# Choosing experts ahead of prompt attention, with four or five slot pairs of each chunk moved into it

## The chip, the cores and the metric

The kernel runs on one core of a Trainium2 chip. The metric is device time in microseconds, the median of three timed executions. Beside them stands one execution taken with the hardware profiler, from which all rows below come. Engine names are those of the profile: PE is TensorE, PEld its weight loads, DVE is VectorE, ACT is ScalarE, POOL is GpSimd (here it only issues DMAs), SP is SyncE (it issues the weight tiles and other large loads).

## The reference

One decoder layer over 1024 prompt tokens and 8 x 4 new tokens. What matters here is its last part, a retrieval of experts for each token:

```python
q = (xb @ w_query).reshape(PEER_BLOCK, PEER_HEADS, PEER_KEY_DIM)        # 8 heads
s1 = einsum('thd,hkd->thk', q[..., :half], sub_keys[:, 0])              # 128 scores
s2 = einsum('thd,hkd->thk', q[..., half:], sub_keys[:, 1])              # 128 scores
v1, i1 = top_k(s1, 16); v2, i2 = top_k(s2, 16)
cand = v1[..., :, None] + v2[..., None, :]                              # 256 candidates
sv, si = top_k(cand, 16)
eidx = take_along_axis(cidx, si)                                        # 16 experts
gate = softmax(sv)
act = gelu(einsum('thkd,td->thk', expert_u[eidx], xb))
out = einsum('thk,thkd->td', gate * act, expert_v[eidx])
```

Ahead of it stand one combined input projection, differential attention (8 heads, causal), an S5 state-space branch with a gated linear unit, two gated projections, an output projection, and rmsnorms. All is float32.

## The kernel before

**Chunks and stages.** After a front part (norm, S5 scan) the tokens are taken in three chunks: blocks 0 and 1; blocks 2 to 4; blocks 5 to 7 with the new tokens. A chunk runs through the stages glu, s5, v, att, dec (the last chunk alone), ga, out and query. In chunk 0 attention comes first and has no retrieval beside it. Each stage is a block of its own: all engines meet at its end. glu, s5, ga and query multiply weight tiles of 128x1024 (8 or 16 a stage, loaded by SP) with the chunk's 384 or 416 columns.

**Retrieval beside the stages.** Blocks 0, 1, 2, 3, the new tokens, 6 and 7 are "gathered". For each of 50 "heads" (a block's head g) 16 slots are worked off in 8 pairs, 400 pairs in all. A slot is one expert row per token: POOL gathers 128 rows of 8 KB (1 MB) into a ring of 8 buffers, DVE makes the dot product (`u_dot`, L1130), ACT the gelu and the weight (L1221, L1230), and DVE adds the weighted row (`v_add`, L1140). `dve_step(p)` does the two dots of pair p and the two additions of pair p-1. Blocks 4 and 5 are worked densely in a last stage, over all 128 x 128 experts, with the pairs from 240 on beside it.

**Where the pairs lie.** `PAIR_PLAN` says how many pairs each stage takes, by an order written by hand; `share` spreads them over the steps of the stage. After unit n of attention (one head of attention and one block of 128 queries; 24 units a chunk) the pairs up to `27 * (n + 2) // 24` of the stage have been done in chunk 1, so that some units take two pairs and the others one. In glu and s5 the pairs up to `n_pairs * (j + 1) // 8` come ahead of DVE's product for tile or tile pair j.

**Choices.** Before the slots of head g can be gathered, DVE must choose its 16 experts (`choose`, `top_pairs`, parts 0 to 5, a chain of 13 links, L1047 to L1093). Head g+2 is chosen beside the pairs of head g, part r behind pair 8g + r:

```python
if r < 6 and g + 2 < HEADS:
    choose(dve, g + 2, r)
```

The results (idx, tops, gates, gsum, ntop) lie in buffers of 4 heads. POOL loads the scores of head g from DRAM 8 pairs ahead of its choice (`step_scores`, `load_scores`).

**Attention on DVE and ACT.** In unit n DVE makes the probabilities (L1834, L1836, L1840), the first dot and addition of its pair (`begin_pair`), the maxima of the next unit (L1827), and then the rest of its pair or pairs; at the middle unit of each head of attention in chunks 1 and 2 it also normalises the head before (L1851, L1853). ACT takes in the output of the unit before (L1739), copies the turned probabilities (L1776), makes the next unit's exponentials (L1731), the roots (L1750), takes in a key or query tile (L1712, L1716), and then the pairs' gelus and weights.

Of the kernel before, what the change touches and what calls it, by code (L numbers as in the profile page):

```python
# [15 lines left out]
U32 = mybir.dt.uint32  # L16
# [28 lines left out]
ARENA = 52992  # L45
# [11 lines left out]
def hybrid_step(nc, dr, out):  # L57

    root = ExitStack()
    with root:  # L60
# [418 lines left out]
        with nc.Block() as block:  # L479
# [138 lines left out]
            def _(sp):  # L618
# [9 lines left out]
                for b in range(2):  # L628
# [11 lines left out]
                     (7, 14, 9, 27, 0, 14, 7, 18),  # L640
                     (8, 15, 10, 28, 40, 15, 8, 16))
# [204 lines left out]
        RING, AHEAD, KCH = 8, 6, 13  # L846
# [95 lines left out]
        for g in range(2, HEADS):  # L942
            assert scores_kept(g) or step_scores(g) <= HALF * (g - 2), (g, step_scores(g))
# [40 lines left out]
        def gather(pool, s):  # L984
# [3 lines left out]
            if s >= RING:  # L988
# [3 lines left out]
                                    bass.IndirectOffsetOnAxis(ap=idx[:, g % 4, j:j + 1], axis=0)  # L992
# [31 lines left out]
        def head_job(g):  # L1024
            return g + sum(step < HALF * (g - 2) for step in DENSE_STEP)

        def dense_job(d):
            return d + DENSE_STEP[d] // HALF + 3
# [51 lines left out]
        def choose(dve, g, part):  # L1080
            if part < 5:
# [9 lines left out]
                top_pairs(dve, head_job(g), part, mine, tops[:, g % 4, :], e12)  # L1091
            else:
                nc.vector.scalar_tensor_tensor(idx[:, g % 4, :], e12[:, 0, :], float(PK), e12[:, 1, :],  # L1093
# [24 lines left out]
        def gate_norm(dve, g):  # L1118
            dve.wait_ge(ex_d, g + 1)
            nc.vector.reciprocal(gsum[:, g % 4:g % 4 + 1], gsum[:, g % 4:g % 4 + 1]).then_inc(gt_v, 1)  # L1120
# [56 lines left out]
        def dve_step(dve, p):  # L1177
# [12 lines left out]
            if r < 6 and g + 2 < HEADS:  # L1190
                choose(dve, g + 2, r)
# [7 lines left out]
        def gate_exp(act, g):  # L1199
            act.wait_ge(tk_done, g + 1)  # L1200
            nc.scalar.activation(ntop[:, g % 4:g % 4 + 1], tops[:, g % 4, 0:1], ACT.Copy, scale=-1.0).then_inc(nt_d, 1)
            act.wait_ge(nt_d, g + 1)
            nc.scalar.activation(gates[:, g % 4, :], tops[:, g % 4, :], ACT.Exp, bias=ntop[:, g % 4:g % 4 + 1],
                                 accum_out=gsum[:, g % 4:g % 4 + 1]).then_inc(ex_d, 1)

        def gate_scale(act, g):
            act.wait_ge(gt_v, g + 1)
            nc.scalar.activation(gates[:, g % 4, :], gates[:, g % 4, :], ACT.Copy, scale=gsum[:, g % 4:g % 4 + 1]).then_inc(gs_d, 1)
# [1586 lines left out]
```

## Time and profile before

| | |
|---|---|
| median of 3 runs | 4130.23 us (4128.51 to 4132.54) |
| profiled execution | 4135.06 us, of which the span from first to last instruction is 4133.2 us |
| mean granted TensorE clock | 0.909 |
| PE busy | 3444.7 us (83%) |
| DVE busy | 3099.4 us (75%) |
| ACT busy | 1516.5 us (37%) |
| mean DMA rate | 317 GB/s |
| gathers of expert rows (L991) | 800 |

A share of busy time is a mean over stages with different limits, so the table says little on the stages that the change touches; the rows further down are by stage. The stages' bounds in the trace, in microseconds: glu of chunk 1 from 742 to 796.8, s5 to 900.3, v to 953.9, attention to 1208.3, ga to 1315.3, out to 1383.8, query to 1517.3; chunk 2: glu to 1571.7, s5 to 1682.8, v to 1743.8, attention to about 2031. The dense tiles run from 3094 to the end at 4133.2.

### The profile page before, as it was taken

Reading aid. Unit: us, or ns where it says so; the run is one execution under the profiler, and the core shown is the slowest. Engines: PE = TensorE matmul, PEld = TensorE weight load, DVE = VectorE, ACT = ScalarE, POOL = GpSimd, SP = SyncE. Lnnn points to the kernel's source line nnn. Section 1 sums busy time; section 2 is a strip of 40 time slices with the busy share of each in tenths; the row PEclk is TensorE's granted clock in tenths of the full one; section 3 lists DMA queues with packets and bytes.
Section 4 is the critical chain, followed back from the end, with each engine's and each line's share of the span. In section 5 each row is a group of like instructions: output and inputs, shape, how many; then the busy total and the mean of one; then the engine's idle time right before and its main releaser. Section 6 shows DMA issues by size and latency. Waiting matters only on the chain. (4 is left out here: it accounts for less than half of the span.)

```text
span 4133.2 us, 48907 instructions
## 1 busy us (share of the span) xinstructions
PE 3444.7 (83%) x15862; PEld 2286.7 (55%) x15862; DVE 3099.4 (75%) x6443; ACT 1516.5 (37%) x3644; POOL 1057.2 (26%) x880
## 2 busy tenths in 40 slices
PE   7988997887778688888677848884779999999998
PEld 5756875544444344355466634343436666666665
DVE  6584112788978778889876878899978887788775
ACT  2232521434763234266533323323433333233232
POOL 0100001332223333412222233332323333332331
PEclk9999998998989889998887869897989999999999
DMA  3032456998879999978798979987999999999996
GB/s 140 4 97 99 140 174 248 352 418 318 318 267 416 353 390 389 412 259 287 273 388 338 362 303 387 333 323 246 376 354 370 416 416 416 415 416 417 413 412 243
DMA packets 312800, 1311.93 MB, mean 317 GB/s; under 512 B 39586, under 2 KB 115842, under 8 KB 206178
## 3 DMA queue, kind: packets, MB, share of 16 engines
q0 software_dynamic: 120320, 854.80, 52.5%
q1 hardware_dynamic: 191842, 453.87, 29.4%
q8 instruction: 128, 2.10, 0.2%
q14 instruction: 126, 1.03, 0.1%
q10 hardware_dynamic: 384, 0.13, 0.0%
HBM read 1250.07 MB, written 56.79 MB: 316 GB/s over the span
## 5 line engine op out<-in xcount | busy, mean ns | idle before, releaser
L991 POOL DMA_INDIRECT arena<-in_uv,arena x800 | 1001.4, 1252 | 2324.9 <-DVE arena L1140 2088.4
L695 PE MATMUL ps<-arena 128*128 128x256 f32 (+2 forms) x3456 | 1107.0, 480 | 148.4 <-DMA arena<-in_w_stat 69.6
L1130 DVE CUSTOM_DVE_ANT_0 arena<-arena 128x1024 f32<-128x1024 f32 x800 | 972.7, 1219 | 52.2 <-DMA arena<-in_uv,arena 35.7
L1140 DVE SCALAR_TENSOR_TENSOR arena<-arena 128x1024 f32<-128x1024 f32 x736 | 942.5, 1281 | 86.9 <-ACT arena L1230 86.0
L695 PEld LDWEIGHTS ps<-arena 128*128 128x128 f32 x3456 | 676.3, 199 | 535.5 <-issue 361.4
L1221 ACT ACTIVATE arena<-arena 128x2 f32<-128x2 f32 x400 | 81.0, 203 | 1136.8 <-DVE arena L1130 1095.9
L2542 PE MATMUL ps<-arena 128*128 128x256 f32 x2048 | 470.9, 384 | 0.0
L2551 PE MATMUL ps<-arena 128*128 128x512 f32 x1024 | 460.1, 592 | 0.5 <-DMA arena<-in_uv 0.5
L2542 PEld LDWEIGHTS ps<-arena 128*128 128x128 f32 x2048 | 385.2, 193 | 48.9 <-issue 0.5
L2551 PEld LDWEIGHTS ps<-arena 128*128 128x128 f32 x1024 | 194.4, 190 | 192.2 <-issue 185.8
L2656 DVE TENSOR_TENSOR arena<-arena 128x256 f32<-128x256 f32 x128 | 79.8, 624 | 253.1 <-ACT arena L2621 222.2
L1221 ACT ACT_TABLE_LOAD x138 | 177.1, 1283 | 56.2 <-PEq L1394 23.3
L1230 ACT ACTIVATE arena<-arena 128x1 f32<-128x1 f32 x800 | 192.0, 287 | 13.5 <-ACT arena L1221 0.6
L2531 PEld LDWEIGHTS ps<-ident,arena 128*128 128x128 f32 x1024 | 121.0, 143 | 109.9 <-issue 81.4
L2531 PE MATMUL ps<-ident,arena 128*128 128x128 f32 x1024 | 136.9, 278 | 39.4 <-ACT arena L2596 22.9
L2244 PE MATMUL ps<-arena 128*128 128x512 f32 (+1 forms) x288 | 129.6, 611 | 24.9 <-PEq L1394 14.5
L2596 ACT ACTIVATE arena<-ps 128x512 f32<-128x512 f32 x256 | 135.9, 580 | 33.6 <-PE ps L2531 19.6
L1982 PE MATMUL ps<-arena 128*64 128x128 f32 x1024 | 145.5, 303 | 0.0
L1827 DVE TENSOR_REDUCE arena<-ps 128x1 f32<-128x384 f32 (+5 forms) x128 | 90.8, 751 | 68.6 <-PE ps L1640 68.3
L2021 PE MATMUL ps<-ident,arena 128*128 128x128 f32 x512 | 83.8, 311 | 69.9 <-DMA arena<-in_cache_k 40.9
L1982 PEld LDWEIGHTS ps<-arena 128*64 128x64 f32 x1024 | 129.4, 154 | 13.6 <-issue 10.5
L307 PE MATMUL ps<-arena 128*128 128x512 f32 (+1 forms) x288 | 126.2, 600 | 4.2 <-PEq L118 4.2
(296 smaller groups left out, 4101.5 us busy)
## 6 DMA issues: line engine op xcount, KB each, us to landing
arena<-in_uv SPq DMA_DIRECT2D x256, 512.0 KB
arena<-in_w_stat SPq DMA_DIRECT2D x216, 512.0 KB
arena<-in_cache_k SPq DMA_DIRECT2D x64, 512.0 KB
arena<-in_cache_v SPq DMA_DIRECT2D x64, 512.0 KB
arena<-in_w_mov SPq DMA_DIRECT2D x14, 2048.0 KB, 13.1
scr_w<-arena SPq DMA_DIRECT2D x16, 1024.0 KB, 19.6
arena<-scr_w SPq DMA_DIRECT2D x16, 1024.0 KB
arena<-in_uv,arena POOLq DMA_INDIRECT x800
```

Source lines behind the costliest of these rows:

```text
L695: last = nc.tensor.matmul(ps[:, bank, 0:w], wbuf[m % NWB][:, kc * P:(kc + 1) * P], moving[:, kc, :], start=(kc == 0), stop=(kc == KC - 1))
L991: pool.indirect_dma_start(ring[s % RING], None, dr["uv"], bass.IndirectOffsetOnAxis(ap=idx[:, g % 4, j:j + 1], axis=0)).then_inc(row_in[s ...
L1130: nc.vector.tensor_tensor_reduce(ring[s % RING][:, 0:D], ring[s % RING][:, 0:D], h2r[:, b % 2, :], 1.0, 0.0, ALU.mult, ALU.add, act_in[:, ...
L1140: nc.vector.scalar_tensor_tensor(accr[:, b % 2, :], ring[s % RING][:, D:2 * D], wgt[:, s % RING:s % RING + 1], accr[:, b % 2, :], ALU.mult ...
L1221: nc.scalar.activation(act_out[:, p % 2, :], act_in[:, k:k + 2], ACT.Gelu).then_inc(gelu_d, 1)
L1230: last = nc.scalar.activation(wgt[:, k + q:k + q + 1], gates[:, g % 4, 2 * r + q:2 * r + q + 1], ACT.Copy, scale=act_out[:, p % 2, q:q + 1])
L1982: last = nc.tensor.matmul(flat_s[:, p * P:(p + 1) * P], qpad[:, h * ROWS:(h + 1) * ROWS], kT[:, n % 2, h, :], start=(h == 0), stop=(h == H ...
L2244: last = nc.tensor.matmul(ps[0:rows, 2 * (b % 2) + k, :], mT[:, kc, (b - b0) * P:(b - b0) * P + rows], o_slab[:, k, kc, :], start=(kc == 0 ...
L2531: last = nc.tensor.transpose(ps[:, 6 + i // 4, (i % 4) * P:(i % 4 + 1) * P], u_rows[:, e % NUR, i * P:(i + 1) * P], ident[:, :])
L2542: last = nc.tensor.matmul(ps[:, 4 + e % 2, 0:2 * P], u_turned[:, e % 2, kc, :], h2d[:, kc, :], start=(kc == 0), stop=(kc == KC - 1))
L2551: last = nc.tensor.matmul(ps[:, 2 * j + k, :], wgt_t[:, e % NW, j * P:(j + 1) * P], v_rows[:, e % NV, 512 * k:512 * (k + 1)], start=(e == ...
L2596: nc.scalar.activation(u_turned[:, e % 2, 4 * i:4 * i + 4, :].rearrange("p c n -> p (c n)"), ps[:, 6 + i, :], ACT.Copy).then_inc(turn_free, 1)
```

## The change

The plan moves pairs and choices; no operation is added or left out. In chunk 1 glu, s5, v and ga take one pair less each and attention four more; in chunk 2 glu takes one less, s5 two, v one, and attention four more. The boundaries before chunk 1's glu (4), at chunk 1's end (100), after chunk 2's attention (161) and at the end of chunk 2 (240) stay.

Each choice now takes four successive pairs rather than six (`CHOICE_PARTS`), from a step given by `CHOICE_STEP`. For heads 2 to 10 and 15 to 22 the steps are written out, for the others they are 8(g-2) as before. So heads 3 to 8 are all chosen between pairs 6 and 29, ahead of chunk 1's attention (pairs 31 to 61), heads 9 and 10 in ga; heads 15 to 21 between pairs 100 and 127, ahead of chunk 2's attention (129 to 160), and head 22 from its last pair on. Results are kept for 8 heads, the ring of diagonal matrices (`diag`, used by pairs 240 to 271) shrinks from 4 to 3, and scores are loaded 6 pairs ahead of their choice.

```diff
-ARENA = 52992
+ARENA = 53040
...
         PAIR_PLAN = ((0, 0, 0, 0, 0, 0, 0, 4),
-                     (7, 14, 9, 27, 0, 14, 7, 18),
-                     (8, 15, 10, 28, 40, 15, 8, 16))
+                     (6, 13, 8, 31, 0, 13, 7, 18),
+                     (7, 13, 9, 32, 40, 15, 8, 16))
...
-        RING, AHEAD, KCH = 8, 6, 13
+        RING, AHEAD, KCH, CHOSEN, NDIAG = 8, 6, 13, 8, 3
...
-        idx, tops, gates, gsum = take([4, TOPK], U32), take([4, TOPK]), take([4, TOPK]), take([4])
-        ntop = take([4])
+        idx, tops, gates, gsum = take([CHOSEN, TOPK], U32), take([CHOSEN, TOPK]), take([CHOSEN, TOPK]), take([CHOSEN])
+        ntop = take([CHOSEN])
...
-        diag, spread, ss8 = take([4, P]), take([NS]), take([1])
+        diag, spread, ss8 = take([NDIAG, P]), take([NS]), take([1])
...
+        CHOICE_PARTS = ((0,), (1,), (2, 3), (4, 5))
+        BEFORE_ATT = (0, 6, 10, 14, 18, 22, 26, 62, 66), (100, 104, 108, 112, 116, 120, 124, 160)
+        CHOICE_STEP = [-2, -1] + [HALF * (g - 2) for g in range(2, HEADS)]
+        CHOICE_STEP[2:11], CHOICE_STEP[15:23] = BEFORE_ATT
+
         def step_scores(g):
-            return (-2, -1, -1)[g] if g < 3 else max(HALF * (g - 3), PAIRS_BEFORE[chunk_of(GATHERED[head_block(g)]) + 1])
+            return (-2, -1, -1)[g] if g < 3 else max(CHOICE_STEP[g] - 6, PAIRS_BEFORE[chunk_of(GATHERED[head_block(g)]) + 1])
...
         def head_job(g):
-            return g + sum(step < HALF * (g - 2) for step in DENSE_STEP)
+            return g + sum(step < CHOICE_STEP[g] for step in DENSE_STEP)
...
-            if r < 6 and g + 2 < HEADS:
-                choose(dve, g + 2, r)
+            for n in range(2, HEADS):
+                if 0 <= p - CHOICE_STEP[n] < len(CHOICE_PARTS):
+                    for part in CHOICE_PARTS[p - CHOICE_STEP[n]]:
+                        choose(dve, n, part)
...
                         n = v_before_pe[p] + q
-                        if n >= 4:
-                            act.wait_ge(v_pe, n - 3)
-                        nc.scalar.activation(diag[:, n % 4, 0:m], pattern, ACT.Copy, scale=wgt[:, k + q:k + q + 1]).then_inc(diag_d, 1)
+                        if n >= NDIAG:
+                            act.wait_ge(v_pe, n - NDIAG + 1)
+                        nc.scalar.activation(diag[:, n % NDIAG, 0:m], pattern, ACT.Copy, scale=wgt[:, k + q:k + q + 1]).then_inc(diag_d, 1)
```

## Rows read from the trace of the kernel before

**Rows 1.** Windows by stage: bounds and length, busy us by engine, PEclk, DMA share, GB/s

```profile
751.30:796.80 45.50, 35.48 (x111) 20.56 (x109) 44.32 (x81) 28.89 (x48) 18.93 (x15) 0.91 0.93 369
796.80:900.30 103.50, 91.31 (x257) 52.35 (x258) 83.12 (x147) 39.32 (x78) 36.64 (x30) 0.91 0.97 391
900.30:953.90 53.60, 41.31 (x96) 18.00 (x96) 51.79 (x95) 14.11 (x43) 25.91 (x19) 0.93 1.01 408
953.90:1208.30 254.40, 189.00 (x816) 120.34 (x816) 216.09 (x422) 170.66 (x385) 57.23 (x57) 0.86 0.83 296
1208.30:1315.30 107.00, 86.91 (x256) 50.12 (x257) 89.53 (x165) 36.85 (x73) 36.96 (x31) 0.91 0.92 371
1526.60:1571.70 45.10, 38.40 (x110) 20.54 (x109) 43.16 (x80) 27.28 (x44) 18.86 (x15) 0.95 1.00 403
1571.70:1682.80 111.10, 96.10 (x257) 51.24 (x257) 91.18 (x164) 38.90 (x80) 38.95 (x32) 0.91 0.97 392
1682.80:1743.80 61.00, 57.17 (x128) 22.23 (x129) 59.18 (x105) 22.83 (x58) 29.94 (x23) 0.97 1.01 412
1743.80:2031.00 287.20, 229.98 (x1101) 152.65 (x1101) 248.46 (x441) 191.71 (x389) 60.45 (x61) 0.89 0.78 276
3094.00:4133.20 1039.20, 1006.02 (x4083) 694.40 (x4081) 786.64 (x1361) 317.03 (x868) 313.80 (x250) 0.99 0.97 394
```

**Rows 2.** DVE's waits: glu 1, s5 1, ga 1, glu 2, s5 2 (us, times, longest)

```profile
DVE arena L1381 <- ACT arena L1373: 9.5, 1, 9.5
...
DVE arena L1445 <- PE ps L695: 13.2, 3, 7.7
DVE arena L1130 <- DMA arena<-in_uv,arena: 5.3, 7, 1.2
...
DVE arena L1447 <- PE ps L695: 8.1, 2, 7.8
DVE arena L1130 <- DMA arena<-in_uv,arena: 7.8, 5, 2.8
...
DVE arena L1381 <- ACT arena L1373: 2.3, 1, 2.3
...
DVE arena L1130 <- DMA arena<-in_uv,arena: 10.1, 8, 2.4
```

**Rows 3.** Timeline of DVE: one pair, then a choice, then the next

```profile
2787.70 1.23 DVE L1130 CUSTOM_DVE_ANT_0 arena<-arena 128x1024 f32<-128x1024 f32 x1
...
2792.39 0.48 DVE L1047 MAX8 arena<-arena 128x8 f32<-128x128 f32 x2
...
2794.61 0.09 DVE L1058 MATCH_VALUE_LOAD arena<-arena 128x8 f32 x1
...
2798.05 0.17 DVE L1069 TENSOR_SCALAR arena<-arena 128x16 uint32<-128x16 uint32 x1
...
2800.73 0.49 DVE L1047 MAX8 arena<-arena 128x8 f32<-128x128 f32 x2
```

**Rows 4.** Windows of single attention heads, two of chunk 1, one of chunk 2

```profile
1026.60:1061.50 34.90, 24.54 (x96) 16.17 (x98) 32.20 (x63) 21.27 (x50) 8.43 (x8) 0.81 0.84 294
1061.50:1084.70 23.20, 21.62 (x106) 13.60 (x102) 21.80 (x39) 19.58 (x43) 4.69 (x5) 0.99 0.88 315
1831.70:1859.60 27.90, 25.80 (x138) 17.15 (x136) 25.41 (x40) 21.37 (x41) 4.68 (x5) 1.00 0.81 285
```

**Rows 5.** Timeline of DVE and ACT, a middle unit without choice, chunk 2

```profile
1841.37 1.22 DVE L1130 CUSTOM_DVE_ANT_0 arena<-arena 128x1024 f32<-128x1024 f32 x1
...
1850.71 0.18 DVE L1851 RECIPROCAL arena<-arena 128x3 f32<-128x3 f32 x1 [2.25 <-ACT arena L1750]
...
1851.10 1.28 ACT L1221 ACT_TABLE_LOAD   x1
1852.40 0.20 ACT L1221 ACTIVATE arena<-arena 128x2 f32<-128x2 f32 x1
1852.63 0.48 ACT L1230 ACTIVATE arena<-arena 128x1 f32<-128x1 f32 x2
```

More of the change, by code:

```diff
@@ L942, in hybrid_step @@
         for g in range(2, HEADS):
-            assert scores_kept(g) or step_scores(g) <= HALF * (g - 2), (g, step_scores(g))
+            assert scores_kept(g) or step_scores(g) <= CHOICE_STEP[g], (g, step_scores(g))
+            assert (g == 2 or CHOICE_STEP[g - 1] + len(CHOICE_PARTS) <= CHOICE_STEP[g]) and CHOICE_STEP[g] <= HALF * (g - 1) - 2 and g - CHOICE_STEP[g] // HALF < CHOSEN
         def load_scores(pool, g):
@@ L1024, in head_job @@
         def head_job(g):
-            return g + sum(step < HALF * (g - 2) for step in DENSE_STEP)
+            return g + sum(step < CHOICE_STEP[g] for step in DENSE_STEP)
         def dense_job(d):
-            return d + DENSE_STEP[d] // HALF + 3
+            return d + sum(step <= DENSE_STEP[d] for step in CHOICE_STEP)
         assert sorted([head_job(g) for g in range(HEADS)] + [dense_job(d) for d in range(2 * PH)]) == list(range(HEADS + 2 * PH))
@@ L1090, in choose @@
                     dve.wait_ge(loaded, n)
-                top_pairs(dve, head_job(g), part, mine, tops[:, g % 4, :], e12)
+                top_pairs(dve, head_job(g), part, mine, tops[:, g % CHOSEN, :], e12)
             else:
-                nc.vector.scalar_tensor_tensor(idx[:, g % 4, :], e12[:, 0, :], float(PK), e12[:, 1, :],
+                nc.vector.scalar_tensor_tensor(idx[:, g % CHOSEN, :], e12[:, 0, :], float(PK), e12[:, 1, :],
                                                ALU.mult, ALU.add).then_inc(tk_done, 1)
@@ L1200, in gate_exp @@
             act.wait_ge(tk_done, g + 1)
-            nc.scalar.activation(ntop[:, g % 4:g % 4 + 1], tops[:, g % 4, 0:1], ACT.Copy, scale=-1.0).then_inc(nt_d, 1)
+            nc.scalar.activation(ntop[:, g % CHOSEN:g % CHOSEN + 1], tops[:, g % CHOSEN, 0:1], ACT.Copy, scale=-1.0).then_inc(nt_d, 1)
             act.wait_ge(nt_d, g + 1)
-            nc.scalar.activation(gates[:, g % 4, :], tops[:, g % 4, :], ACT.Exp, bias=ntop[:, g % 4:g % 4 + 1],
-                                 accum_out=gsum[:, g % 4:g % 4 + 1]).then_inc(ex_d, 1)
+            nc.scalar.activation(gates[:, g % CHOSEN, :], tops[:, g % CHOSEN, :], ACT.Exp, bias=ntop[:, g % CHOSEN:g % CHOSEN + 1],
+                                 accum_out=gsum[:, g % CHOSEN:g % CHOSEN + 1]).then_inc(ex_d, 1)
         def gate_scale(act, g):
             act.wait_ge(gt_v, g + 1)
-            nc.scalar.activation(gates[:, g % 4, :], gates[:, g % 4, :], ACT.Copy, scale=gsum[:, g % 4:g % 4 + 1]).then_inc(gs_d, 1)
+            nc.scalar.activation(gates[:, g % CHOSEN, :], gates[:, g % CHOSEN, :], ACT.Copy, scale=gsum[:, g % CHOSEN:g % CHOSEN + 1]).then_inc(gs_d, 1)
         def act_step(act, p):
@@ L1229, in act_step @@
                 for q in range(2):
-                    last = nc.scalar.activation(wgt[:, k + q:k + q + 1], gates[:, g % 4, 2 * r + q:2 * r + q + 1], ACT.Copy,
+                    last = nc.scalar.activation(wgt[:, k + q:k + q + 1], gates[:, g % CHOSEN, 2 * r + q:2 * r + q + 1], ACT.Copy,
                                                 scale=act_out[:, p % 2, q:q + 1])
@@ L1272, in pe_step @@
                 for c in range(2):
-                    last = nc.tensor.matmul(ps[0:m, 6 + c, :], diag[:, n % 4, 0:m],
+                    last = nc.tensor.matmul(ps[0:m, 6 + c, :], diag[:, n % NDIAG, 0:m],
                                             ring[s % RING][:, D + 512 * c:D + 512 * (c + 1)],
```

4 lines of the change are left out of this document (2 added, 2 removed).

## The prediction

> **What bounds the kernel now.** I read the page first (PE 83%, DVE 75%, both means over unlike stages), then windows cut at the bounds of the stages, then the waits of DVE in them, and at last the timeline of attention, unit by unit. In the windows [rows 1] three things are to be seen. The dense tiles from 3094 on are PE's: 1006.0 of 1039.2 us busy. No pair is moved into or out of them, so I take them as fixed, with all from pair 161 on. Second, from glu of chunk 1 to v of chunk 2, DVE is busy 80 to 97% of each stage and the DMA engines move 370 to 412 GB/s at a share near 1. Third, attention runs the DMA engines at 0.83 and 0.78 and DVE at 85 and 87%. So there is room for transfers in attention, and hardly any on DVE ahead of it.
>
> Every stage ends with a meeting of all engines, so the last engine sets each stage by itself. In glu and v that is DVE: glu of chunk 1 is 44.3 of 45.5 us busy after its first tile. In s5 and ga DVE is also last, but idles 20.4 and 17.5 us [rows 1]: for the first product of PE (part of 13.2 and 8.1 us) and for gathered rows (5.3, 7.8 and, in s5 of chunk 2, 10.1 us) [rows 2].
>
> **The prices.** A pair is 4.69 us of DVE when nothing holds it (2787.70 to 2792.39). A choice is 8.34 us (2792.39 to 2800.73): 2.2 for part 0, 3.4 for parts 1 and 2, 2.7 for 3 to 5 [rows 3]. The choices of gathered heads add part 5, one small operation; I take 8.4. Both DVE totals stay; only their place changes, and with it what hides them.
>
> **The change, stage by stage** (from the lists of pairs and choice steps of either plan).
> - Query of chunk 0: the last parts of head 2 now come behind pair 3, ahead of the block's end: +1.9 us.
> - Glu 1: one pair less; choices 8.4 for the 7.9 before. DVE is the last engine, and PE, 35.5 us busy in the same stretch, leaves room: -4.2.
> - s5 1: one pair less (-4.7), choices 27.4 where there were 13.4 (+14.0). Of this the first part 0 (2.2) now lies in the wait for the first product, and DVE's other waits, 5.5 for PE and 5.3 for rows, mostly go (8.4 of 10.8): -1.3. If none went it would be +7.1.
> - v 1: -4.7 and +4.7: 0.
> - ga 1: one pair less, choices +8.8 (head 9 whole, part 3 of head 11), 2.2 of it in the first wait, and of 7.8 us for rows I take half away: -2.0; with all waits kept +1.9.
> - Query 1: head 14 is ended there, behind its last pair and with DVE the last engine: +1.5.
> - Glu 2: this is the surprise. With 8 pairs, `share` puts one ahead of the first product, where DVE waits only 2.3 us more; with 7 it puts none there (7 // 8 = 0), and DVE waits some 9.5 as in glu 1 [rows 2]. Behind the first product stand 7 pairs in both plans, but 14.5 us of choices for 6.2: +8.3.
> - s5 2: two pairs less (-9.4), choices +11.2; of the 10.1 us for rows I take 6.6 away: -4.8, with waits kept +1.8.
> - v 2: -4.7 and +5.7: +1.0.
>
> **Attention** decides the rest. It loses 27.9 us of choices in chunk 1 (from part 3 of head 6 to head 9; part 2 lay in the wait before the first maxima) and 25.2 in chunk 2, and gets four pairs in each. By DVE's sum that is -9.1 and -6.4. But a head without choices is not DVE's alone: 23.2 us with DVE 21.8 and PE 21.6 busy in chunk 1, 27.9 with 25.4 and 25.8 in chunk 2 [rows 4]. PE and ACT are at their limit too, and choices now fill waits. The extra pairs become second pairs of a unit. In a middle unit of chunk 2 the probabilities are done at 1841.37, and ACT has its exponentials, roots and a query tile to do before it can load the gelu table at 1851.10 and give the weights at 1852.63 + 0.48 [rows 5]. The first addition of a second pair waits for these weights. It can start at 1853.3; two additions, a dot and the 2.3 us from L1851 to the next first dot (row 1850.71, whose wait of 2.25 us is then gone) put the next unit at 1859.2, where it was 1853.05. So a second pair in a middle unit costs 6.1 us, not 4.7. The same reckoning gives 6.0 for middle units of chunk 1, 5.9 for first and 5.0 for last ones.
>
> In chunk 1 the second pairs rise from 3 to 7, net 22.9 us. A head with one second pair (5.9) and 6.1 us of choices takes 34.9 us, 11.7 over the free one [rows 4]: there a choice gave 0.95 of its length, so 26.5 go: -4 (bounds -9 and +3). In chunk 2 `32 * k // 24` puts all second pairs into middle units, one a head where every other head had one: 4 x 6.1 = +24.4. A choice there fills first what the free head idles (2.5 us), so I take 0.7 of its length: 25.2 x 0.7 = 17.6. That is +7 (bounds -6 and +11).
>
> On the price of the table load the Trainium skill (ScalarE: Activation LUTs, What ACT_TABLE_LOAD costs) says about 1283 ns plus some 1380 ns of drain for each change of set. The trace agrees on the first and shows no drain: the load at 1851.10 takes 1.28 and the gelu starts at 1852.40 [rows 5]. By the page each of the 8 new second pairs would wait 1.4 us longer, +11 us in all; the row decides.
>
> **What I cost at nothing.** Attention's first wait (part 2 of head 6 lay in it). Scores loaded 6 instead of 8 pairs ahead, and only 4 ahead for head 16 and 2 for head 3, whose choices come early: POOL issues them ahead of that step's gathers, and at 5 us a pair or more 2 pairs are 10 us; cover gone, DVE would wait once or twice some 5 us. POOL's wait for choices gets shorter, since every choice ends earlier. Three diagonals for four: ACT waits for PE at most a pair earlier, in a stretch where PE takes them microseconds later; 0 to +2. Choices in four steps instead of six elsewhere: same work.
>
> **Sum.** +1.9 -4.2 -1.3 +0 -2.0 +1.5 +8.3 -4.8 +1.0 is +0.4 outside attention, -4 and +7 in it: +3.4 us. The profiled execution's 4135.1 (span 4133.2 and 1.9 around it) becomes 4138.5; it lies 4.8 over the median of 4130.2, which becomes **4133.6**.
>
> **The rivals.**
> - *Attention is DVE's after all.* Second pairs cost 4.7 and choices give all back: -9.1 and -6.4 where I have -4 and +7, so 18.5 less: 4115. For it: DVE is 94% busy in the free head of chunk 1. Against: the 2.25 us wait.
> - *Bytes rule ahead of attention.* Eight pairs leave the stages ahead of it, at 2.1 MB each and 0.41 MB/us 5.1 us apiece: -41, and attention takes them into its free DMA time: about 4090. For it: the share near 1 [rows 1]. Against: DVE waited for rows only 5 to 10 us a stage [rows 2]. The Trainium skill (Perfetto Trace Analysis, Optimization Strategy) says that interleaving regimes with different most-contended engines can improve performance; here that would be this case.
> - *A second pair costs more* (slower). If ACT gives the weights 1.8 us later than reckoned, since PE's tile is late at a lower clock (0.81 in the head of 34.9 us, 0.99 in the free one [rows 4]), eight new ones bring +14: 4148. With my sum at +3.4 it decides from some 6.6 us a second pair on.
> - *The relief does not come* (slower). DVE gets 34.0 us more of choices in both s5 and ga, and its waits for rows and PE stay: 8.4, 6.6 and 3.9 over my terms: 4152. It decides from 5 of these 19 us on.
> - *Nothing to be seen*: my sum is itself within 0.2% (8.3 us), about what a measurement of this kernel can tell from no change, so this is no case apart.
>
> **How the numbers follow.** My sum 0.49 (of it 0.40 within 0.2%, 0.05 faster, 0.04 slower); DVE's attention 0.20 (0.18 faster); bytes 0.06; dearer second pairs 0.14 (0.12 slower); no relief 0.11 (0.10 slower). That is faster 0.29, same 0.45, slower 0.26. The range takes in the first and third rival, 4111 to 4149; my sum alone would be 4123 to 4144.
>
> **What would show it.** Attention of chunk 1 near 250 us and of chunk 2 near 294 (254.4 and 287.2 now); a wait of L1140 for ACT L1230 in nearly every unit with two pairs, none of 2.25 us at L1851; glu 2 near 63 us with a wait of about 9 us at L1381; s5 2 near 106 with under 4 us for rows. Attention of chunk 2 under 283 us would prove me wrong on second pairs, s5 2 over 111 on the relief.

## The result and the profile after

The changed kernel takes 4183.93 us (median of 4 runs, 4172.27 to 4193.32), the kernel before 4131.39 in the same comparison (4128.51 to 4138.27): a ratio of 1.0116, 95% interval 1.0097 to 1.0135. It is slower by 1.2%, where I forecast 4133.6 and a range up to 4149. The profiled execution is the slowest of the four, 4193.3 us with a span of 4191.5, against 4133.2 before. (Four pairs of each chunk go into attention, 27 to 31 and 28 to 32, not "four or five" as the title has it.)

Windows of the changed kernel at the bounds of its stages (columns as in [rows 1]; glu, s5, v, attention and ga of chunk 1, query of chunk 1, then glu, s5 and v of chunk 2):

```profile
738.30:789.70 51.40, 43.04 (x128) 25.04 (x129) 40.45 (x79) 27.43 (x45) 17.55 (x15) 0.93 0.93 368
789.70:890.60 100.90, 89.39 (x256) 51.41 (x257) 91.20 (x199) 36.95 (x73) 34.70 (x29) 0.92 0.96 386
890.60:945.60 55.00, 43.62 (x96) 18.94 (x97) 51.71 (x104) 13.88 (x41) 20.78 (x16) 0.90 0.94 340
945.60:1215.80 270.20, 195.06 (x817) 124.55 (x817) 207.26 (x335) 173.66 (x397) 70.86 (x64) 0.84 0.85 307
1215.80:1316.60 100.80, 86.69 (x257) 50.09 (x257) 92.66 (x194) 37.40 (x71) 35.03 (x29) 0.94 0.92 371
1384.50:1524.10 139.60, 103.22 (x353) 63.97 (x353) 105.83 (x190) 31.24 (x88) 55.54 (x41) 0.87 1.00 389
1524.10:1585.90 61.80, 47.79 (x128) 25.49 (x128) 50.86 (x113) 30.80 (x50) 19.88 (x17) 0.86 0.86 331
1585.90:1690.40 104.50, 95.84 (x257) 51.05 (x257) 91.52 (x191) 39.99 (x76) 35.72 (x29) 0.94 0.93 372
1690.40:1752.10 61.70, 56.94 (x128) 22.21 (x129) 58.54 (x122) 15.52 (x45) 23.47 (x18) 0.97 0.94 344
```

The stages outside attention sum to little, as forecast: 4.2 us less from query of chunk 0 to v of chunk 2. Attention of chunk 1 grew from 254.4 [rows 1] to 270.2. Chunk 2's attention has no clean bound in the trace, so I compare both from the first unit's probabilities to the last unit's. The kernel before:

```profile
973.00:1196.40 223.40, 167.99 (x752) 107.63 (x752) 206.36 (x401) 161.69 (x364) 54.61 (x55) 0.88 0.84 302
1764.10:2020.20 256.10, 207.45 (x1026) 138.74 (x1026) 239.73 (x427) 182.97 (x370) 58.35 (x59) 0.90 0.79 277
```

The changed kernel:

```profile
964.10:1203.90 239.80, 174.79 (x752) 112.18 (x752) 199.27 (x321) 164.59 (x375) 67.39 (x62) 0.86 0.86 312
1772.70:2053.20 280.50, 219.24 (x1026) 149.37 (x1026) 238.07 (x356) 198.26 (x394) 74.41 (x65) 0.86 0.80 282
```

The case is in these four lines. DVE has less to do in both (199.3 for 206.4, 238.1 for 239.7), as my sum had it, and yet they are 16.4 and 24.4 us longer. DVE waits more. And the 1026 products of PE in chunk 2's line take 219.2 us instead of 207.5, at a granted clock of 0.86 instead of 0.90: the same work has grown.

Where the profiled executions differ, in us (after minus before): ahead of the change -3.4; stages outside attention as far as v of chunk 2 -4.2; attention of chunk 1 +15.9; attention of chunk 2 +24.4 and decode +3.2; ga, out and query of chunk 2 up to pair 240 +4.5; pairs 248 to 274 +17.8; everything behind 0. That is 58.2 of a difference of 58.3 in the spans. Pairs 248 to 274 lie beside the grid stage, the one ahead of the dense tiles, in which results of ACT are stored into the DRAM tensor scr_w.

DVE's waits in chunk 2 between those bounds, before:

```profile
DVE arena L1140 <- ACT arena L1230: 7.6, 8, 2.1
DVE arena L1851 <- ACT arena L1750: 4.5, 2, 2.3
```

and after (lines moved by 6 and 8):

```profile
DVE arena L1146 <- ACT arena L1238: 34.4, 15, 3.7
DVE arena L1842 <- ACT arena L1739: 5.0, 12, 1.5
```

The additions wait 26.8 us more for ACT's weights. Every middle unit of chunk 2 now has two pairs: 8 units, where the kernel before had 4 (in chunk 1 it is 7 for 3). One of them, DVE:

```profile
1856.12 1.29 DVE L1146 SCALAR_TENSOR_TENSOR arena<-arena 128x1024 f32<-128x1024 f32 x1 [1.10 <-ACT arena L1238]
1857.43 2.36 DVE L1835 TENSOR_REDUCE arena<-ps 128x1 f32<-128x1024 f32 x2
...
1867.01 1.29 DVE L1146 SCALAR_TENSOR_TENSOR arena<-arena 128x1024 f32<-128x1024 f32 x1 [3.66 <-ACT arena L1238]
...
1872.94 1.22 DVE L1136 CUSTOM_DVE_ANT_0 arena<-arena 128x1024 f32<-128x1024 f32 x1
```

and ACT beside it:

```profile
1862.53 0.20 ACT L1739 ACTIVATION_READ_ACCUMULATOR arena<-ps,arena 128x1 f32 x1
...
1863.04 1.28 ACT L1758 ACT_TABLE_LOAD   x1
1864.33 0.21 ACT L1758 ACTIVATE arena<-arena 128x3 f32<-128x3 f32 x1
1864.44 0.50 ACT L1724 ACTIVATE arena<-ps 128x416 f32<-128x416 f32 x1
1864.96 1.28 ACT L1229 ACT_TABLE_LOAD   x1
1866.25 0.20 ACT L1229 ACTIVATE arena<-arena 128x2 f32<-128x2 f32 x1
1866.49 0.48 ACT L1238 ACTIVATE arena<-arena 128x1 f32<-128x1 f32 x2
```

From the maxima (1857.43) to the next unit's dot (1872.94) are 15.51 us. In the free unit of the kernel before the maxima start at

```profile
1843.71 2.35 DVE L1827 TENSOR_REDUCE arena<-ps 128x1 f32<-128x1024 f32 x2
```

and the prediction put the next dot at 1859.2 with a second pair, so 15.5 us. That part of the reckoning held to 0.1 us. The Trainium skill's drain behind a table load (ScalarE: Activation LUTs, What ACT_TABLE_LOAD costs), which by its figure would have made it an estimated 1.4 us more, is again not there: load at 1864.96, gelu at 1866.25. What I had missed lies around it. Windows of the changed kernel over another head's two-pair unit (1925.7 to 1944.8), its beginning and its last part, and over the unit behind it:

```profile
1925.70:1930.00 4.30, 4.30 (x24) 2.56 (x22) 3.06 (x6) 2.97 (x8) 0.71 (x1) 1.00 1.05 370
...
1940.00:1944.80 4.80, 0.93 (x8) 0.52 (x4) 4.28 (x8) 4.45 (x11) 2.10 (x2) 0.80 0.46 155
1944.80:1953.30 8.50, 5.70 (x26) 5.33 (x27) 8.24 (x15) 4.71 (x8) 1.92 (x3) 0.51 0.81 307
```

and PE's longest wait in the head from 1907.7 on:

```profile
PE ps L1670 <- DVE arena L1848: 5.6, 1, 5.6
```

While DVE waits for weights and makes up the second pair, PE has no new probabilities to turn (transpose, L1670): it idles 5.6 us at a stretch (0.9 us busy of the last 4.8). Behind that idle stretch the granted clock falls from 1.00 to 0.51, which is its lower level of 1.2 GHz nearly throughout, and the next unit starts with slow products. The same eight turning products take 1.97 us there and 1.04 in the free head before; and in the middle unit of the next head ACT, which has to take in PE's key or query tile ahead of the gelu, waits for it:

```profile
1837.48 1.97 PE L1670 MATMUL ps<-ident,arena 128*128 128x128 f32 x8 [5.57 <-DVE arena L1848]
1853.54 0.52 ACT L1720 ACTIVATE arena<-ps 128x416 f32<-128x416 f32 x1 [1.09 <-PE ps L695]
```

```profile
1853.43 1.04 PE L1662 MATMUL ps<-ident,arena 128*128 128x128 f32 x8
```

(The first two are the changed kernel's, the last is the free head's.) PE begins the products of that tile 3.55 us into the head, where it was 2.23 in the free one, and the difference of 1.3 us is handed on to ACT and to DVE's first addition, the 1.10 us above. In the free head before, the clock stayed at 1.00 and PE had 25.8 of 27.9 us to do [rows 4]; now a head of chunk 2 takes 36.1 us on the mean, and PE is 30.4 us busy in the one from 1907.7 to 1944.8. So the second pair costs 8.2 us over a free head: the 6.1 of the reckoning, some 1.3 in its own unit (1.10 ahead of the first addition) and 0.8 in the two others. How much of these 2.1 us is the idle stretch itself and how much the low clock behind it, the runs don't separate.

### The profile page after: what moved, and what is told of

The parts are those of the page before. It is cut to its first block and busy times, and to the rows that moved or that the text cites. A ratio compares the mean times of both kernels' runs of the same rounds, so it can differ in the third digit from the quotient of the medians.

```text
span 4191.5 us, 48844 instructions
## 1 busy us (share of the span) xinstructions
PE 3473.5 (83%) x15862; PEld 2312.9 (55%) x15862; DVE 3103.0 (74%) x6443; ACT 1525.7 (36%) x3649; POOL 1081.2 (26%) x880
## 5 line engine op out<-in xcount | busy, mean ns | idle before, releaser
L997 POOL DMA_INDIRECT arena<-in_uv,arena x800 | 1025.2, 1281 | 2361.3 <-DVE arena L1146 2122.6
L1229 ACT ACT_TABLE_LOAD x141 | 180.9, 1283 | 62.1 <-PEq L1402 32.2
L2029 PE MATMUL ps<-ident,arena 128*128 128x128 f32 x512 | 83.9, 312 | 66.8 <-DMA arena<-in_cache_k 36.9
## 6 DMA issues: line engine op xcount, KB each, us to landing
arena<-in_w_mov SPq DMA_DIRECT2D x14, 2048.0 KB, 13.6
arena<-in_uv,arena POOLq DMA_INDIRECT x800, 10.8
```

Source lines behind the costliest of these rows:

```text
L997: pool.indirect_dma_start(ring[s % RING], None, dr["uv"], bass.IndirectOffsetOnAxis(ap=idx[:, g % CHOSEN, j:j + 1], axis=0)).then_inc(row_ ...
L1229: nc.scalar.activation(act_out[:, p % 2, :], act_in[:, k:k + 2], ACT.Gelu).then_inc(gelu_d, 1)
```

## The experiments

The table has the lengths that the texts below speak of, from one profiled execution each: attention from first to last probabilities, the stages ahead (chunk 1: glu, s5, v, ga; chunk 2: glu, s5, v) and query 1, in us. The medians of the kernel before lay between 4129.7 and 4134.4 us in the different comparisons; the ratios are to the one of the same comparison.

| kernel | attention 1 | attention 2 | ahead, chunk 1 | query 1 | ahead, chunk 2 | median, ratio to before (95%) |
|---|---|---|---|---|---|---|
| before | 223.4 | 256.1 | 318.5 | 133.5 | 226.5 | |
| choices alone | 211.2 | 249.8 | 327.7 | 139.4 | 238.4 | 4151.7, 1.0039 (1.0021 to 1.0058) |
| pairs alone | 255.4 | 294.1 | 299.0 | 133.0 | 209.7 | 4163.1, 1.0071 (1.0043 to 1.0099) |
| changed | 239.8 | 280.5 | 308.1 | 139.6 | 228.0 | 4183.9, 1.0116 (1.0097 to 1.0135) |
| changed, gelu earlier | 220.9 | 258.7 | 307.5 | 142.0 | 223.0 | 4143.5, 1.0007 (0.9987 to 1.0027) |
| pairs alone, gelu earlier | 244.6 | 278.5 | 297.9 | 132.5 | 210.8 | 4141.1, 1.0015 (1.0002 to 1.0029) |
| before, gelu earlier | 220.2 | 251.8 | 317.9 | 130.0 | 225.0 | 4130.6, 0.9984 (0.9966 to 1.0002) |
| one pair a unit | 201.2 | 230.0 | 331.9 | 134.0 | 226.8 | 4110.9, 0.9943 (0.9922 to 0.9963) |

### The two halves of the change

Choices alone is the changed kernel with the old plan of pairs; pairs alone is the kernel before with the new one.

```diff
-                     (6, 13, 8, 31, 0, 13, 7, 18),
-                     (7, 13, 9, 32, 40, 15, 8, 16))
+                     (7, 14, 9, 27, 0, 14, 7, 18),
+                     (8, 15, 10, 28, 40, 15, 8, 16))
```

> The changed kernel with the old plan of pairs: only the choices are moved (and the three diagonals kept). Theory 1, cover: a choice beside a second pair lay in the wait of the first addition for ACT's weights and was nearly free there, so taking it out gives little: attention of chunk 2 falls only some 7 us (287.2 to about 280), that of chunk 1 some 16 (254.3 to about 238); the stages ahead of them gain some 28 us over the changed kernel; with the 20 us of the stretch of pairs 240 to 272 the total is about 4155. Theory 2, the prediction's 0.95 and 0.7 of a choice: attention falls by 26 and 18 us (to 228 and 270), total about 4135.

> The kernel before with the new plan of pairs: the choices stay beside the pairs of head g-2. Theory 1, cover: a second pair costs some 8.5 us in a unit whether or not choices lie there, and the choices lie in the wait, so attention comes out about as in the changed kernel or 0 to 10 us a chunk longer (270 to 280 and 311 to 322). Theory 2, the prediction's sum: a second pair costs 6.1 and the choices come on top: 254.3 + 23 = 277 and 287.2 + 24 = 311. What tells them apart is the difference to the changed kernel in chunk 2's attention: 18 us by theory 2, under 8 by theory 1. Glu of chunk 2 near 62 us by both. Total about 4165 (theory 1), 4172 (theory 2).

Windows of choices alone:

```profile
983.90:1195.10 211.20, 165.41 (x752) 107.06 (x752) 180.84 (x296) 161.44 (x364) 53.90 (x54) 0.91 0.87 315
1781.20:2031.00 249.80, 205.22 (x1026) 136.97 (x1026) 216.88 (x327) 182.96 (x369) 58.73 (x56) 0.92 0.80 285
```

Windows of pairs alone:

```profile
953.10:1208.50 255.40, 176.66 (x752) 113.45 (x752) 230.99 (x453) 164.84 (x375) 65.19 (x63) 0.84 0.82 294
1754.10:2048.20 294.10, 217.63 (x1026) 149.13 (x1026) 264.92 (x468) 198.14 (x394) 71.64 (x68) 0.84 0.78 272
```

Both halves cost time, and together they cost what they cost singly. Taking the choices out gives 12.2 us in chunk 1 and 6.3 in chunk 2 at the old plan, and 15.6 and 13.6 at the new one. Their DVE time is 27.9 and 25.2 us, so about half comes back at best and a quarter at worst. Four pairs more cost 32.0 and 38.0 us where choices lie beside them, and 28.6 and 30.7 where none do: 7.2 to 9.5 us each. Theory 1 had choices alone right (a stage of 242.0 us for its 238; the stretch from v's end to pair 161's first dot 289.8 for before's 296.5); in pairs alone it was too strong: that stretch is 333.4, 12.5 us over the changed kernel's 320.9, between its 8 and theory 2's 18.

The cover of theory 1 can be read head by head. In chunk 2 of the kernel before, three heads have a second pair and 6.4 to 6.9 us of choices each; they take 36.7, 36.9 and 38.1 us, and with the choices moved away 35.0, 34.8 and 35.0. So a choice there gave back 0.3 to 0.5 of its length, and the middle units themselves, 54.5 us in all, became 55.3. Over chunk 2's attention the wait for the weights grows from 7.6 to 21.5 us where DVE's work falls by 22.9:

```profile
DVE arena L1146 <- ACT arena L1238: 21.5, 12, 3.7
```

But it depends on the place in the unit. In pairs alone three middle units have their choice (2.2 us) only behind the second pair, after the wait; there the wait is 3.66 us as in the changed kernel, and they take 21.25 us where the changed kernel takes 19.03: the choice comes on top in full. Only what lies ahead of the second pair's first addition can fill the wait. These three units are 6.7 of the 13.6 us that the choices gave beside the new plan, where they gave 6.3 beside the old.

Ahead of attention pairs alone wins 36.3 us over the stages of the table, a mean of 4.5 for each of the eight pairs. The mean hides a spread: one pair less gave 4.3 us in glu 1, 8.5 in s5 1, 2.3 in ga 1 and nothing in glu 2, and two gave 12.8 in s5 2, where DVE's waits for rows fell from 10.1 to 1.1 us and those for PE rose from 7.8 to 19.1. So in s5 a pair is worth more than DVE's 4.69 us, and these stages are not shown to be DVE's alone. Choices alone loses 9.2 + 5.9 + 11.9 = 27.0 us there, and 18.5 come back in attention: a choice is dearer where it goes than where it leaves.

Glu of chunk 2 is a clean check of one term: 61.8 us in the changed kernel, 62.1 with the choices alone, 54.8 with the pairs alone (54.5 before). The pair that leaves it brings nothing, as its place is taken by a wait; the choices bring all of the 7.3.

### ACT gives the weights earlier

In a unit with two pairs ACT works the first of them off right behind the exponentials, ahead of the roots and the key or query tile.

```diff
+                        if share(c, "att", n + 1, N) - done_pairs["act"] == 2:
+                            peer_act(act, done_pairs["act"] + 1)
                         if rooted(n) is not None:
                             roots(rooted(n))
```

> The changed kernel, but in a unit with two pairs ACT does the gelu and the weights of the first of them right behind the exponentials, ahead of the roots and of the key or query tile. Theory 1: the weights come 2.1 us earlier in the middle units of chunk 2, the wait of 3.7 us ahead of the second pair's first addition falls to about 1.5, the stretch to pair 161 falls by 8 x 2 = 16 us, attention of chunk 1 by 5 to 12; total 4155 to 4165. Theory 2 (what waits is only moved, since PE gets its key and query tiles taken in later and the roots come later): within 5 us.

Waits of DVE between the probabilities of chunk 2's first and last unit:

```profile
DVE arena L1146 <- ACT arena L1238: 16.0, 14, 1.8
```

Windows, same bounds as above:

```profile
967.80:1188.70 220.90, 169.65 (x752) 109.64 (x752) 198.70 (x320) 167.93 (x378) 67.49 (x62) 0.89 0.91 337
1756.10:2014.80 258.70, 208.59 (x1026) 137.48 (x1026) 236.73 (x355) 203.34 (x398) 74.33 (x65) 0.93 0.85 306
```

Timeline of a middle unit, DVE and ACT:

```profile
1834.97 2.36 DVE L1837 TENSOR_REDUCE arena<-ps 128x1 f32<-128x1024 f32 x2
...
1840.57 1.28 ACT L1229 ACT_TABLE_LOAD   x1
...
1842.62 1.28 DVE L1146 SCALAR_TENSOR_TENSOR arena<-arena 128x1024 f32<-128x1024 f32 x1 [1.74 <-ACT arena L1238]
```

Theory 1 holds and is outdone: 40 us, where I expected some 25. The weights come 7.65 us behind the maxima instead of 9.58, the wait falls from 3.66 to 1.74, and with PE idle for less time the clock is 0.93 instead of 0.86 and PE's 1026 products take 208.6 us again, not 219.2. DVE's work in the stretch is unchanged within 1.4 us. The edit is a swap in one engine's order. It adds a table load to units in which the second gelu would have found its table loaded (65 loads for 61 in the stretch, ACT 203.3 us busy for 198.3); ACT has the time.

The same edit on the kernel before and on pairs alone tells whether the choices had been cover:

> The kernel before with the earlier gelu on ACT in units with two pairs (3 in chunk 1, 5 in chunk 2), nothing else. Theory 1: of the some 20 us that the edit took from each attention of the changed kernel, with 7 and 9 such units, it takes as much for each such unit here, 2.2 to 2.7 us: 18 to 20 us in all, 4112 to 4116 where the kernel before has 4132. Theory 2, cover: here half of the units with two pairs have choices, which fill the wait for the weights, and the edit brings only what waits are left (L1140 for L1230, 0.5 to 2.1 us a unit in the rows): 8 units by about 1, total 4122 to 4128.

> The new plan of pairs with the choices where they were and with the earlier gelu. Theory 1 (ACT's late weights made a second pair dear): with them early it costs some 5 us, so attention comes to about 264 and 300 to pair 161 (286.3 and 333.4 without), against 38 us won ahead of it; total 4163 - 38 = 4125. Theory 2, cover: the choices lay partly in that wait, so of what the edit gave the changed kernel (18.1 and 20.2 us) only half is to be had: 4140 to 4148.

It takes 3.2 and 4.3 us from the two attentions of the kernel before (3 and 4 units with two pairs), 10.8 and 15.6 with the pairs alone (7 and 8), and 18.9 and 21.8 in the changed kernel (also 7 and 8; the expectations had one too many for chunk 2). Per unit that is some 1.1, 1.8 and 2.7 us. So choices beside a two-pair unit lay in the wait for ACT and were in part free there: theory 2 in both runs. In the times before, gelu earlier is within the uncertainty of before (4130.6, ratio 0.9984, interval up to 1.0002), a little over the 4122 to 4128 of theory 2; pairs alone, gelu earlier fits its 4140 to 4148 (4141.1).

### Second pairs in the last unit of a head

```diff
-            return PAIRS_BEFORE[c] + sum(PAIR_PLAN[c][:s]) + PAIR_PLAN[c][s] * min(i + 1, n) // n
+            return PAIRS_BEFORE[c] + sum(PAIR_PLAN[c][:s]) + min(PAIR_PLAN[c][s], (PAIR_PLAN[c][s] * min(i + 1, n) + (16 if stage == "att" and n > 1 else 0)) // n)
```

> The changed kernel with the second pairs of attention in the last unit of a head (no roots and no query tile on ACT there) instead of the middle one. Theory 1 (a second pair is dear because it must wait for weights that ACT gives behind the exponentials, the roots and the query tile): a second pair costs 5 to 6 us instead of 7.8 in chunk 2, the wait of L1146 for L1238 falls from 4.9 us a unit to under 3, and the stretch from 1752 to pair 161 falls from 320.9 to 300 to 305; chunk 1 falls by 0 to 10; total 4160 to 4170. Theory 2 (the price is that of PE's and DVE's work at their joint limit, wherever the pair lies): within 5 us of the changed kernel.

DVE's waits in chunk 2's attention:

```profile
DVE arena L1146 <- ACT arena L1238: 26.1, 15, 2.5
DVE arena L1859 <- ACT arena L1758: 9.7, 6, 2.4
```

In chunk 2 this formula puts the second pairs into the last unit of seven heads and one more pair ahead of the first unit; in chunk 1, with its 31 pairs, they come to lie in first, middle and last units (0, 3, 6, 10, 13, 17 and 20), so only chunk 2 tests the place. Attention is 4.6 and 9.2 us shorter (235.2 and 271.3), less than theory 1 has: of the 34.4 us of waits for weights 8.3 go, but the normalisation in the middle units, which a second pair had covered, waits 9.7 us for the roots again. In the time nothing is to be seen: 4182.7 us (ratio to before 1.0101, 1.0067 to 1.0134), with one execution of 6966.7 us left out of the ratio. The place matters less than the order on ACT.

### One pair a unit

Pairs go the other way: 24 in each attention.

```diff
-                     (7, 14, 9, 27, 0, 14, 7, 18),
-                     (8, 15, 10, 28, 40, 15, 8, 16))
+                     (7, 15, 9, 24, 0, 15, 8, 18),
+                     (8, 15, 10, 24, 44, 15, 8, 16))
```

> The kernel before with pairs moved the other way, choices as they were: attention 24 pairs in both chunks (one a unit, no second pairs), the three of chunk 1 to s5, ga and out, the four of chunk 2 to dec. Theory 1 (a second pair costs 7 to 9 us in attention and 4.7 at most elsewhere): attention of chunk 1 about 230 (254.3), up to pair 156's unit end in chunk 2 about 37 us less, the other stages +3 x 4.7 and +4 x 4.7 at most: total 4100, between 4095 and 4110. Theory 2 (a second pair costs 6.1, and the choices on top keep their price): 4117 to 4122.

```profile
978.50:1179.70 201.20, 165.28 (x752) 105.70 (x752) 188.98 (x373) 155.83 (x346) 46.55 (x49) 0.92 0.85 305
1750.90:1980.90 230.00, 200.41 (x1026) 132.56 (x1026) 218.06 (x390) 179.79 (x356) 46.53 (x50) 0.97 0.78 273
```

22.2 and 26.1 us go: 7.4 and 6.5 a pair with all choices in place. They cost 7.4 us in s5 and 6.4 in ga of chunk 1, out even falls by 3.7; the four in decode cost 21.3 (attention and decode together 726.1 for 730.9), 5.3 each, more than I had allowed. The total is 4110.9, 11 above my figure, just over its bound of 4110, and 0.57% below the kernel before. The clock of chunk 2's attention is 0.97. A kernel with 24 pairs in chunk 1 and the old 28 in chunk 2, with the earlier gelu, was the candidate from both results:

> Candidate: chunk 1 with 24 pairs in attention (three more in s5, ga and out), chunk 2 as before, and the earlier gelu for the 5 units with two pairs there. Chunk 1 brought 9.4 us by the stages of the run with one pair a unit (22.6 off attention, 13.2 on s5, ga and out); the gelu brings 5 to 12. Total 4110 to 4118.

It takes 4108.3 us (4100.8 to 4115.1), ratio 0.9940 (0.9922 to 0.9959), a little under the 4110 to 4118 expected, with attentions of 197.0 and 253.3 us. It is 0.6% faster than the kernel before and some 75 us under the changed one, but it can't be told from one pair a unit (0.9943).

### Four steps for a choice

Query of chunk 1 grew by 6.1 us in the changed kernel and by 5.9 with the choices alone, not with the pairs alone. Four steps instead of six in the kernel before, with the scores loaded 6 pairs ahead, and the scores by themselves:

```diff
-            if r < 6 and g + 2 < HEADS:
-                choose(dve, g + 2, r)
+            if r < 4 and g + 2 < HEADS:
+                for part in ((0,), (1,), (2, 3), (4, 5))[r]:
+                    choose(dve, g + 2, part)
```

> The kernel before with every choice in four steps instead of six and scores loaded 6 pairs ahead, every start as before. Theory A: this is what lengthened query of chunk 1 (133.5 to 139.6) and pairs 248 to 274 (209.8 to 227.6, and 223.2 with the choices alone): both come back, total about 4145. Theory B: query 1's loss comes from head 14's end alone and is there (+3 to +6), but pairs 248 to 274 differ by when the stores meet the gathers, not by the choices' steps: 205 to 225 in no relation to the edit, total 4130 to 4138.

> The kernel before with scores loaded 6 pairs ahead of their choice instead of 8, choices in six steps as they were. The kernel with both edits took 0.45% more (4150 for 4134; query of chunk 1 141.5 for 133.5). Theory A: it is the scores: POOL's load stands ahead of other gathers, and query 1 is again near 141, total 0.3 to 0.5% more. Theory B: it is the four steps, which put parts 2 to 5 into two pairs, so that a pair's dots and with them ACT's weights come later where PE waits for weight tiles: here no change, query 1 133 to 134, total within 0.2%.

DVE's waits in query 1 with four steps:

```profile
DVE arena L1140 <- ACT arena L1231: 33.8, 9, 8.9
```

and with the scores alone:

```profile
DVE arena L1140 <- ACT arena L1230: 27.0, 6, 9.5
```

With four steps query 1 takes 141.5 us and the kernel 0.45% more (4150.2 for 4134.4, ratio 1.0045, 1.0028 to 1.0062), near the 4145 of theory A; with the scores alone 133.4 and 4130.7 (0.9998, 0.9978 to 1.0017). So it is the steps: 16 us by the medians, of which query 1 has 8.0, with 6.7 us more of waits for weights, in a stage in which PE itself waits for weight tiles. Of the rest the profiled execution, at 4139.3 its fastest of nine, shows only a part (2.7 from pair 161 to 232, 3.1 in pairs 248 to 274). Six steps given back to heads 11 to 13 and from 23 on in the changed kernel:

> The changed kernel with six steps again for the choices of heads 11 to 13 and from 23 on; the moved ones keep their four. Theory A: four steps beside pairs that wait for ACT cost what the kernel with them alone lost: query of chunk 1 falls from 139.6 to 134 to 137, decode and the last query stage by a few, total 0.2 to 0.4% less, 4168 to 4176. Theory B: they cost only by head 14, which ends at the barrier of query 1 and stays so here: within 0.2%.

Query 1 is back at 135.0 us, but the time, 4171.2 (1.0093, 1.0056 to 1.0129), can't be told from the changed kernel's; that execution's attentions are 5 us longer each, with a lower clock. So of the whole loss about 5 us are shown to be the steps' in query 1; the medians of this pair of kernels differ by 13, and the next part shows where the other microseconds may lie.

### Pairs 248 to 274

This stretch, with the stores into scr_w, was 17.8 us longer in the profile after, and the ring of diagonals is used in it.

```diff
-        RING, AHEAD, KCH, CHOSEN, NDIAG = 8, 6, 13, 8, 3
+        RING, AHEAD, KCH, CHOSEN, NDIAG = 8, 6, 13, 8, 4
...
-        diag, spread, ss8 = take([NDIAG, P]), take([NS]), take([1])
+        diag, spread, ss8 = lay(23808, [NDIAG, P]), take([NS]), take([1])
```

> The changed kernel with four diagonals instead of three, laid into a part of the arena that the grid stage doesn't use. Theory A: the third-for-fourth diagonal ties ACT to PE's product of the pair before (13 waits of ACT L1248, 8.7 us) and this costs most of the 18 us that pairs 240 to 272 lost: the time falls by 12 to 20 us, to about 4168. Theory B: the stretch lost its time to the stores into scr_w, which ACT waits for, and the number of diagonals has no part in it: within 4 us of the changed kernel.

> The kernel before with three diagonals instead of four and nothing else. Theory A (three diagonals cost the stretch of pairs 240 to 272 its 18 us): 4145 to 4151. Theory B (the stores): within 4 us of the kernel before.

> The changed kernel once more, unedited. Theory A, the length of pairs 248 to 274 is the kernel's: 225 to 230 us again (227.6). Theory B, it is the execution's (when the stores into scr_w meet the gathers): another value from the 203 to 228 that the other kernels showed. Attention's two stretches 266 to 271 and 320 to 322 us by either.

The ring has no part in it that can be measured: 4176.7 us with four (1.0110, 1.0075 to 1.0146), and 4132.3 before with three (0.9996, 0.9972 to 1.0019). The stretch itself in the kernel before, the changed one and the same changed kernel again:

```profile
2898.50:3100.00 201.50, 152.84 (x602) 81.14 (x603) 171.93 (x578) 72.90 (x198) 57.16 (x54) 0.89 0.97 364
```

```profile
2938.80:3158.30 219.50, 155.56 (x602) 82.67 (x603) 172.12 (x578) 76.42 (x204) 60.17 (x54) 0.83 0.90 336
```

```profile
2945.00:3150.10 205.10, 153.56 (x602) 82.27 (x603) 171.40 (x577) 75.86 (x204) 58.36 (x54) 0.86 0.95 358
```

(from pair 249's first dot; from 248's they are 209.8, 227.6 and 213.7.) The same kernel shows 14 us less, so a good part of the 17.8 us can belong to the execution; theory B for this run. (Attention repeats: 235.9 and 279.9 us for 239.8 and 280.5.) Yet the sixteen profiled executions are not scattered at random. From 248's first dot to 274's they take, by the number of steps that the choices of these pairs have:

| choices there | kernels | 248 to 274, us | mean |
|---|---|---|---|
| six steps | before, pairs alone, pairs alone gelu earlier, before gelu earlier, one pair a unit, the candidate, scores alone, three diagonals, six steps late | 209.8, 216.8, 206.1, 213.5, 203.5, 203.7, 203.1, 210.4, 205.6 | 208.1 |
| four steps | four steps alone, choices alone, changed, changed again, changed gelu earlier, last unit, four diagonals | 212.9, 223.2, 227.6, 213.7, 213.8, 226.6, 223.8 | 220.2 |

The means are 12 us apart, and only two of the nine reach the lowest of the seven. The kernel with all of the change but six steps here (six late) has 205.6, and the one with four steps and nothing else moved 212.9. So on the mean 12 us go with the four steps, and the rest of the 17.8 with the execution; this is a comparison over kernels that differ in other things too, and which wait the steps lengthen is not shown. It fits the medians: the changed kernel's is 52.5 us over the one before, while its profile shows 40.5 outside this stretch. In the longer execution of the changed kernel ACT waited 68.7 us for its stores into scr_w, the longest 18.1, against 48.4 and 13.2 before; why the stores take longer was not tried.

## Why the prediction was wrong

Its single steps against the profile after:

| step | forecast | measured |
|---|---|---|
| query 0 | +1.9 | -0.8 |
| glu 1, s5 1, v 1, ga 1 | -4.2, -1.3, 0, -2.0 | -3.0, -2.4, +1.2, -6.2 |
| query 1 | +1.5 | +6.1 |
| glu 2, s5 2, v 2 | +8.3, -4.8, +1.0 | +7.3, -6.4, +0.6 |
| attention 1 | -4 (-9 to +3) | +15.9 |
| attention 2 | +7 (-6 to +11) | +24.4, decode +3.2 |
| grid stage | 0 to +2 | +17.8; by sixteen executions some 12 of it with the four steps |

**What held.** The sum outside attention (+0.4, measured -4.2 with out 1's -0.6). Glu 2's rise and its cause: 9.9 us of wait at L1389 (L1381 before) as forecast, and both halves of the change apart confirm the arithmetic. So did two of the signs: waits for the weights in every unit of chunk 2 with two pairs, and s5 2 at 104.5 us without a wait for rows. The relief of DVE's waits came, and more fully than I took it; waits of the changed kernel in ga 1 and s5 1:

```profile
DVE arena L1136 <- DMA arena<-in_uv,arena: 0.5, 1, 0.5
...
DVE arena L1453 <- PE ps L695: 6.1, 2, 4.5
DVE arena L1136 <- DMA arena<-in_uv,arena: 1.2, 1, 1.2
```

against 7.8 us for rows in ga 1, and 13.2 and 5.3 in s5 1 [rows 2]. So the rival "the relief does not come" was wrong, and s5 2 has no wait for rows left.

**First failed step: "I take 0.7 of its length" and "there a choice gave 0.95 of its length".** I priced a choice that leaves by one head against one free head, and set 26.5 and 17.6 us. The runs gave 15.6 and 13.6 beside the new pairs, 12.2 and 6.3 beside the old. A choice beside a two-pair unit filled the wait for ACT's weights, and leaving, it laid the wait bare (7.6 to 21.5 us with the choices alone; 34.4 with the new pairs as well). In one-pair units too only part came back: with the choices alone the middle units of the two heads behind a two-pair one wait 1.2 and 2.5 us for weights, where they waited none. The trace before could have told, by the same three heads of 36.7, 36.9 and 38.1 us. A free head of 27.9 with my own 6.1 on top is 34.0, which leaves 2.7 to 4.1 for the choices, 0.4 to 0.6 of their length, and with the 8.2 measured it leaves 0.6 to 2.0. I compared the choices with the head without a second pair, though the change leaves no head of chunk 2 without one. This step is 10.9 + 4.0 = 15 us.

**Second failed step: "a second pair in a middle unit costs 6.1 us".** On the way from choices alone to the changed kernel it costs 7.7 in chunk 2, on the way from before to pairs alone 9.5; in chunk 1 7.2 and 8.0 for my 5.7. The unit's own chain, from the maxima on, was right to 0.1 us. I left out that PE, which has 25.8 of 27.9 us to do in a free head, idles beside such a unit, that its clock falls to 0.51 in the next, and that late tiles and late exponentials then come back as small waits in all three units. On the path that ends with the choices' removal (pairs first) the step is (32.0 - 22.9) + (38.0 - 24.4) = 22.7 us. Both steps together are 37.6, and the two attentions missed my terms by 16.4 + 4 = 20.4 and 24.4 - 7 = 17.4, 37.8 in all.

**The rivals.** "A second pair costs more" was the right mechanism in the main, PE's tile late at a lower clock and ACT's weights behind it; only it is the weights of the first addition that come late (1.10 us), while those of the second pair came when reckoned. I gave it 0.14 and 7.8 us a pair, and this price fits the choice-free case (7.2 and 7.7); it still ended at 4148, since it kept my worth of the choices. That DVE is attention's bound was refuted by the windows: DVE's work fell and the time rose. Bytes ahead of attention: those stages did shrink by 4.5 us on the mean for each pair that left them (pairs alone), and in s5 by more than DVE's price, so bytes may have a part there; but attention did not take the pairs into free transfer time; there it is the chain through ACT that ends last.

**Third failed step: "Choices in four steps instead of six elsewhere: same work", put at nothing.** The same work, but not the same moments. In the kernel before, four steps by themselves cost 0.45%, 16 us by the medians; in the changed one query 1 shows 6 us, of which I had 1.5, and some 12 more go with the steps in pairs 248 to 274.

The range failed since its bounds were too narrow, not for the way they were added: both attention terms at their upper bounds at once give only 4145. Both attention errors have one cause, the wait for ACT's weights, and so came together.

## What to carry to other kernels

Where work fills a wait, price its removal at the place that will be left, not at a place that is free: a filler that lies ahead of the step that waits may be free, one behind it is paid in full, and taking it away and adding a second item are then not two changes but one. Before moving work into an engine's spare time, read whose result it waits for in each slot and what that engine does first; here the order of two steps on ACT was worth 40 us in the changed kernel, more than the 15.5 that DVE's sum promised for both attentions (9.1 and 6.4). And when a stage is near the limit of PE as well, an idle stretch of PE beside another engine's chain is not free: here the products behind it ran at the lower clock, and some 2 us a head came back as waits. Last, putting the same work into fewer, longer steps is a change of its own and wants its own run: here it cost 16 us.

## What the runs showed of the hardware

- The granted clock follows PE's idle stretches inside a stage: 1.00 over the 14.3 us from 1925.7 to 1940, then 3.9 us of the next 4.8 without a product, then 0.51 over 8.5 us. PE's busy time for chunk 2's 1026 products of attention was 200.4 us at 0.97, 207.5 at 0.90 and 219.2 at 0.86.
- More table loads on ACT (1.28 us each, the function behind one starting within 0.02 us) cost nothing where ACT had the time: 5.0 us more of ACT's work in chunk 2's attention went with 21.8 us less of its length. What counted was which result came first.
- The same kernel profiled twice differed by 14 us in one stretch of 26 pairs with large stores beside gathers (227.6 and 213.7). A difference of that size in two executions says nothing about an edit; that sixteen executions part by the number of steps (means 208.1 and 220.2) says something.
